# A two-layer hybrid encoder step on one core: the cached keys and the convolution rows arrive already turned, and scores run one batch ahead

## What is computed

```python
def _fox_sample(q, k, v, logf, ck, cv, clogf):
    k_all = jnp.concatenate([ck.astype(k.dtype), k], axis=1)      # 512 cached keys, 16 new ones
    v_all = jnp.concatenate([cv.astype(v.dtype), v], axis=1)
    ...
    sc = jnp.einsum('bqhd,bkhd->bhqk', q, k_all, preferred_element_type=jnp.float32) * scale
    sc = sc + cq[..., None] - c_t[:, :, None, :]
    sc = jnp.where(mask, sc, -jnp.inf)
    p = jax.nn.softmax(sc, axis=-1)
    return jnp.einsum('bhqk,bkhd->bqhd', p.astype(v_all.dtype), v_all)

def _layer(...):
    ...
    y_conv, new_conv = _causal_dwconv(u, conv_hist, conv_w)
    x = x + jnp.concatenate([o_ret, o_fox, o_conv], axis=-1) @ w_out
    gate_c, new_ffn = _causal_dwconv(gate_pre, ffn_hist, ffn_conv_w)
    x = x + (jax.nn.silu(gate_c) * (h2 @ w_up)) @ w_down
```

## Time and profile before

| | |
|---|---|
| median of 3 runs | 1590.44 us (1589.42 to 1591.83) |
| the profiled execution, its own time | 1592.12 us |
| its span in the profile | 1590.3 us |
| busy: TensorE | 1569.7 us, 99% |
| busy: VectorE, ScalarE, POOL | 1073.3, 684.6, 398.4 us |
| chain that ended last | TensorE 90%, VectorE 5% |
| DMA | 168.06 MB, mean 106 GB/s |

### The profile page before, as it was taken

One profiled execution on the slowest core, in us unless ns is written; L12 is line 12 of the kernel. 1 busy time (PEld: TensorE's weight loads), 2 busy tenths in 40 slices (PEclk: granted clock), 3 DMA queues, 4 the chain that ended last, 5 costly groups with the idle time before them and its releaser, 6 DMA issues.

```text
span 1590.3 us, 29061 instructions
## 1 busy us (share of the span) xinstructions
PE 1569.7 (99%) x10196; PEld 1375.7 (87%) x10196; DVE 1073.3 (67%) x1847; ACT 684.6 (43%) x1280; POOL 398.4 (25%) x505
## 2 busy tenths in 40 slices
PE   8999999999999999999999999999999999999998
PEld 6878896789999999999888788877899999999997
DVE  4445447539988888888644552675499888878885
ACT  4224327426444444444433233463365444444442
POOL 1113200003433333333112140000044333333330
PEclk9999999999999999999999999999999999999999
DMA  7213455722222233222242235455213222222222
GB/s 230 80 49 91 138 156 192 264 80 67 80 86 86 79 86 88 89 85 73 77 108 67 70 82 180 171 197 203 80 55 117 84 89 79 79 79 79 80 78 72
DMA packets 118872, 168.06 MB, mean 106 GB/s; under 512 B 28261, under 2 KB 80175, under 8 KB 114624
## 3 DMA queue, kind: packets, MB, share of 16 engines
q1 hardware_dynamic: 118648, 166.95, 33.7%
q10 hardware_dynamic: 146, 0.07, 0.0%
HBM read 157.11 MB, written 9.89 MB: 105 GB/s over the span
## 4 chain that ended last, share of the span: by engine, by line
PE 90%; DVE 5%; issue 1%; ACT 1%; DMA 1%; DVEq 1%; POOL 0%; POOLq 0%; SPq 0%; ACTq 0%
PE bank L2239 85%; PE bank L2301 5%; DVE wlo L1538 1%; DVE pf L1898 0%; DMA raw<-in_w_gate 0%; DVE pf L1911 0%; DMA raw<-in_w_in 0%; DVE wlo L1552 0%; DVE xn L1590 0%; DVE x L2026 0%; DVE gulo L1562 0%; DVE gact L2056 0%; DVE hlo L1562 0%; POOLq L1123 0%; POOL s L1121 0%
## 5 line engine op out<-in xcount | busy, mean ns | idle before, releaser
L2239 PE MATMUL bank<-whi,hhi 128*128 128x512 f32 x560 | 225.1, 402 | 0.9 <-DVE hlo L1562 0.6
L2239 PE MATMUL bank<-whi,hlo 128*128 128x512 f32 x560 | 219.3, 392 | 0.0
L2239 PE MATMUL bank<-wlo,hhi 128*128 128x512 f32 x560 | 218.9, 391 | 0.0
L2239 PE MATMUL bank<-hhi,whi 128*128 128x320 f32 x640 | 198.7, 310 | 0.8 <-DVE hlo L1562 0.8
L2239 PE MATMUL bank<-hhi,wlo 128*128 128x320 f32 x640 | 197.8, 309 | 0.0
L2239 PE MATMUL bank<-hlo,whi 128*128 128x320 f32 x640 | 197.6, 309 | 0.0
L1538 DVE TENSOR_TENSOR wlo<-raw,whi 128x1024 fp32r<-128x1024 f32 x80 | 100.0, 1251 | 109.4 <-ACT whi L1156 108.0
L2239 PE MATMUL bank<-whi,guhi 128*128 128x512 f32 x440 | 171.7, 390 | 0.4 <-DVE gulo L1562 0.4
L2239 PE MATMUL bank<-wlo,guhi 128*128 128x512 f32 x440 | 171.3, 389 | 0.0
L2239 PE MATMUL bank<-whi,gulo 128*128 128x512 f32 x440 | 171.3, 389 | 0.0
L2026 DVE TENSOR_TENSOR x<-x,bank 128x512 f32<-128x512 f32 x220 | 142.7, 680 | 29.4 <-PE bank L2239 28.5
(11 more groups left out here) (310 smaller groups left out, 3605.1 us busy)
## 6 DMA issues: line engine op xcount, KB each, us to landing
raw<-in_w_in SPq DMA_DIRECT2D x52, 512.0 KB, 3.9
raw<-in_w_gate SPq DMA_DIRECT2D x44, 512.0 KB, 3.8
raw<-in_w_down SPq DMA_DIRECT2D x44, 512.0 KB, 3.6
vb<-in_cache_fox_v SPq DMA_DIRECT2D x14, 1024.0 KB, 6.8
raw<-in_w_up SPq DMA_DIRECT2D x24, 512.0 KB, 3.8
gains<-in_w_up SPq DMA_DIRECT2D x20, 512.0 KB, 3.7
raw<-in_w_out SPq DMA_DIRECT2D x16, 512.0 KB, 5.7
kb<-in_cache_fox_k SPq DMA_DIRECT2D x6, 1024.0 KB, 4.9
```

The costliest lines, as they stand in the source:

```text
L2239: return pe.matmul(out, lhsT=lhsT, rhs=rhs, start=start, stop=stop, skip_group_check=True)
```

## The change

1. The host lays out `cache_fox_k` with head dimension on partitions and positions along the row, still 8 KB of one batch per partition. `keys_turned`, `key_copy`, `kT` as a destination and `k0` go; `scores` read the loaded buffer itself.
2. History and taps come as one array in the layout of `taps`: one load replaces four, and the transposes, the bank and ScalarE's copy go. In the second layer SP waits for the last history copies of the first (`gpad_hist`) before it.
3. On TensorE scores run one batch further on: `scores(1)` comes before the loop, and step n has `turned(n)`, `scores(n+1)`, `values(n)`. `ss`, `sn` and `pt` alternate between two banks each. VectorE's steps are put as maxima of n+1, then scaling of n−1; ScalarE has exps(0) and exps(1), then in each step the copy of `pt` and exps(n+1).
4. Keys get five homes (the old place of `kT` is one), values four (`vr` lies under `bcr`, the prompt's bias). SP's loads and their waits follow: K3 a little earlier, K4 when the last prompt output is full, then K5, V4, K6, V5, K7, V6, V7 each when the buffer's former content was used. The splits of the `w_out` slabs wait for `so` of batch 3, not 2; ScalarE's come one step later, VectorE's stay in steps 5 to 7 but stand behind the scaling.

```diff
-K_HOME = (0, 1, 2, 3, 0, 1, 0, 1)
-V_HOME = (0, 1, 2, 0, 1, 0, 1, 0)
+K_HOME = (0, 1, 2, 3, 4, 0, 2, 4)
+V_HOME = (0, 1, 2, 3, 0, 2, 3, 0)
...
     if n < NB:
-        jobs += [(("kt", n, p), K_BANKS[(4 * n + p) % 3]) for p in range(4)]
-        jobs += [(("ss", n), 2), (("sn", n), 4)]
+        jobs += [(("ss", n), (2, 0)[n % 2]), (("sn", n), (4, 3)[n % 2])]
     if 1 <= n <= NB:
-        jobs += [(("pt", n - 1), 6), (("so", n - 1), 5)]
+        jobs += [(("pt", n - 1), (6, 1)[n % 2]), (("so", n - 1), 5)]
     if n >= 1:
         jobs.append((("po", n), 7))
...
-        def key_home(n, p_):
-            return kT[:, p_, :] if n > 0 else k0[:, p_, :] if p_ < 2 else kT[:, p_ - 2, :]
-
         oc = ccs
-        kcache = (kb, kbo, kx, ky)
-        vcache = (vb[:, 0], vb[:, 1], vx[:, :, :])
+        kcache = (kb, kx, kbo, ky, kT)
+        vcache = (vb[:, 0], vx[:, :, :], vb[:, 1], vr[:, :, :])
...
-                sp.dma_start(rows[0:16, 0:CW], one("state_conv").rearrange("o b w c -> (o b w) c")).then_inc(rows_in, 16)
-                sp.dma_start(rows[0:16, CW:], one("state_ffn_conv").rearrange("o b w c -> (o b w) c")).then_inc(rows_in, 16)
-                sp.dma_start(rows[16:19, 0:CW], one("conv_w").rearrange("o w c -> (o w) c")).then_inc(rows_in, 16)
-                sp.dma_start(rows[16:19, CW:], one("ffn_conv_w").rearrange("o w c -> (o w) c")).then_inc(rows_in, 16)
+                if l > 0:
+                    sp.wait_ge(gpad_hist, l * PAIRS)
+                sp.dma_start(taps[:, :, :], one("taps").rearrange("o p n -> p (o n)").rearrange("p (c n) -> p c n", c=NCT)).then_inc(taps_in, 16)
...
                 load_k(l, 0)
                 load_v(l, 0)
                 B.wait_full(sp, ("cb_", 1, 1), l)
-                load_k(l, 2)
-                load_v(l, 2)
+                load_k(l, 1)
+                load_v(l, 1)
                 sp.wait_ge(u_last, l + 1)
                 B.wait_taken(sp, ("fs", 5, 1), l)
                 load_bcr(3)
+                load_k(l, 3)
                 sp.wait_ge(cat_lo, l * CATS + 1)
-                load_k(l, 1)
-                load_v(l, 1)
-                load_k(l, 3)
+                load_k(l, 2)
+                load_v(l, 2)
 
                 def next_pb(b):
                     sp.wait_ge(smax, l * NB + b - 3)
                     load_pb(b)
 
-                B.wait_full(sp, ("kt", 0, 3), l)
+                B.wait_taken(sp, ("fs", len(fox_units()) - 1, 1), l)
+                load_v(l, 3)
+                B.wait_full(sp, ("fo", 3), l)
                 load_k(l, 4)
+                B.wait_full(sp, ("ss", 0), l)
+                load_k(l, 5)
                 next_pb(4)
                 B.wait_full(sp, ("so", 0), l)
-                load_v(l, 3)
-                B.wait_full(sp, ("kt", 1, 3), l)
-                load_k(l, 5)
+                load_v(l, 4)
                 next_pb(5)
-                B.wait_full(sp, ("so", 1), l)
-                load_v(l, 4)
+                B.wait_full(sp, ("ss", 2), l)
+                load_k(l, 6)
                 next_pb(6)
-                B.wait_full(sp, ("kt", 4, 3), l)
-                load_k(l, 6)
-                B.wait_full(sp, ("so", 3), l)
+                B.wait_full(sp, ("so", 2), l)
                 load_v(l, 5)
                 next_pb(7)
-                B.wait_full(sp, ("kt", 5, 3), l)
+                B.wait_full(sp, ("ss", 4), l)
                 load_k(l, 7)
+                B.wait_full(sp, ("so", 3), l)
+                load_v(l, 6)
                 B.wait_full(sp, ("so", 4), l)
-                load_v(l, 6)
-                B.wait_full(sp, ("so", 5), l)
                 load_v(l, 7)
 
...
-                evac("taps", taps[:, :, :], l, view=lambda b: b[:, 0:NCT * NTAP].rearrange("p (c n) -> p c n", c=NCT))
...
-                    if n == NU + 2:
-                        evac(("kt", 0, 2), key_home(0, 2), l)
...
-                for n in range(STEPS):
-                    step(n)
+                def exps(n):
+
+                    act.wait_ge(smax, l * NB + n + 1)
+                    o = SB + 8 * (n % 3)
+                    for c0, n_, acc in ((0, PAST, 3), (PAST + NS * n, NS, 4)):
+                        act.activation(ps[:, n % 2, c0:c0 + n_], ps[:, n % 2, c0:c0 + n_], ACT.Exp, scale=-1.0,
+                                       bias=col(o + 2), accum_out=col(o + acc)).then_inc(sexp, 1)
+
+                for n in range(2):
+                    exps(n)
+                for n in range(1, NB + 1):
+                    evac(("pt", n - 1), pTs[:, (n - 1) % 2, 0:512], l)
+                    if n in (5, 6, 7):
+                        B.wait_full(act, ("so", 3), l)
+                        upto(WO + n - 5, l)
+                    if n + 1 < NB:
+                        exps(n + 1)
                 B.wait_taken(act, ("po", STEPS - 1), l)
...
+                def scaled(n):
+                    o = SB + 8 * (n % 3)
+                    dve.wait_ge(sexp, l * 2 * NB + 2 * n + 2)
+                    dve.tensor_tensor(col(o + 5), col(o + 3), col(o + 4), ALU.add)
+                    dve.drain()
+                    dve.reciprocal(col(o + 6), col(o + 5))
+                    dve.drain()
+                    key = ("so", n)
+                    B.wait_full(dve, key, l)
+                    dve.tensor_scalar(ob[:, n % 2, :], bank[B.bank(key)][:, 0:P], col(o + 6), None,
+                                      ALU.mult).then_inc(B.free[B.bank(key)], 1)
+
+                maxima(0)
+                maxima(1)
+                heads_lo(3)
+                for n in range(1, STEPS):
+                    turned_rows(n)
+                    if n + 1 < NB:
+                        maxima(n + 1)
+                    if n <= NB:
+                        scaled(n - 1)
                     if n in (5, 6, 7):
-                        B.wait_full(dve, ("so", 2), l)
+                        B.wait_full(dve, ("so", 3), l)
                         upto(WO + n - 5, l)
-                    if n == 1:
-                        heads_lo(3)
-                    if n >= 1:
...
-                    for p_ in (1, 3) if n == 1 else (2, 3):
-                        B.wait_taken(pe, ("kt", n, p_), l)
+                    wait_cached(pe, k_in, K_HOME, n, l)
                     B.wait_room(pe, past, l)
                     for p_ in range(4):
                         r = slice(32 * p_, 32 * p_ + 32)
-                        ins = mm(bp[r, :], qbd[:, u, r], key_home(n, p_), True, True)
+                        ins = mm(bp[r, :], qbd[:, u, r], kcache[K_HOME[n]][:, p_, :], True, True)
                     fill(ins, past)
 
                 units = fox_units()
...
+                scores(1)
                 for n in range(1, NB):
                     turned(n)
-                    scores(n)
+                    if n + 1 < NB:
+                        scores(n + 1)
                     values(n)
 
```

153 lines of the change are left out of this document (51 added, 102 removed).

## The result

The changed kernel takes 1580.1 us (median of four runs, 1577.8 to 1582.0) where the kernel before took 1590.96 beside it: ratio 0.9932, interval 0.9915 to 0.9949. That is 10.9 us less, where 24.5 were forecast, and outside the range of 1557 to 1577. The profiled execution has a span of 1579.2 us.

A forecast was written before the change was run, and what follows sets the result against it. TensorE, busy 99%, was taken as the bound. 12.1 us a layer gained less 1.5 for transfers, twice, plus 3.3 for the rows, gave 24.5 us less: 1565.9 us, own range 1562 to 1570, wider range 1557 to 1577.

The forecast's parts named there:

- Filter and history rows: Both layers: 24 transposes leave TensorE's queue, 1.65 us a layer, 3.3 us in all.
- Batch 0's key transposes: Start of the cached-batch stage: two transpose groups and a stall before the scores go, 2.5 us less a layer.
- The loop of 3.5 us: Batches 1 to 7: VectorE's maximum and scaled output, then TensorE's transpose and scores, make 3.5 us a batch, against TensorE's 3.0.
- Transfers: Key and value loads inside the stage: at 365 GB/s K7 lands at 290.4, wanted at 289.0; 1.5 us lost a layer.
- The tail: Stage's end: slab splits delay the last steps; scores(6) end at 19.1, first w_out product starts at 28.4 after scores(0).
- Rival B: Cached-batch stage bound by transfers: at 300 GB/s K7 lands 5.7 us late; 1574 us, chance 0.22.
- Rival D: Cached-batch stage: short waits in every batch drop TensorE's clock to the lower level; 1590 us, chance 0.03.
- Rival E: Downstream of the stage: a late slab split or norm gives back half the gain; 1578 us, chance 0.05.
- A: Cached-batch stage: TensorE stays the bound at 3.0 us a batch, K7 ends the stage; 1560 us, chance 0.13.
- C: Cache loads each have the queue alone for 6.8 us, first w_out product 9.3 us late; 1606 us, chance 0.02.

The follow-up runs named there:

- a_nobias: The changed kernel without the loads of the bias tables of batches 4 to 7 (1.05 MB less a layer; measuring only): 1562.3 us.
- c_split: c_v3 with VectorE's split of the second w_out slab moved from the step of batch 6 to that of batch 7: 1561.3 us.
- d_distinct: c_split with the four early bias tables read from 128 different 2 KB rows of the key cache (measuring only): 1560.2 us, one run.
- b_inline: The changed kernel without the look-ahead: each batch's scores computed in its own step again: 1571.0 us.
- b_early: The changed kernel with bias tables 4 to 7 loaded early into their own place, values 3 loaded inside the stage: 1565.6 us.
- b_homes: b_early with keys 5, 6 and 7 in the places of keys 1, 0 and 2, so asked for sooner: 1564.2 us.
- d_same: c_split with the early tables read from 8 rows of the key cache, each for 16 partitions (measuring only): 1562.2 us, one run.
- b_rows8k: b_homes with scratch tables stored head by head, so one load with 8 KB rows brings all four: 1569.6 us.
- d_spread: c_split with the same scratch rows cut by head: eight loads of 16 partitions x 4 rows in place of four: 1562.1 us.
- c_v3: b_homes with values 3 ahead of values 4 in SP's order: 1563.7 us.
- a_order: The changed kernel with only SP's order different: tables 5 and 7, keys 6 and 7 no longer behind value loads 4 and 5: 1575.7 us.
- a_half: The changed kernel loading half of keys 5 to 7 and values 4 to 7, 3.7 MB less a layer (measuring only): 1561.9 us.
- c_rows: The changed kernel with tables 4 to 7 read from 128 different 2 KB rows of the key cache (measuring only): 1567.1 us.

## Why the prediction was wrong

- **Filter and history rows**, −3.3 us: 3.5 measured alone. Right.
- **Batch 0's key transposes**, −2.5 a layer: the end of the first scores moved from 269.79 to 264.68, 5.1 us; 2.4 of it was there before the stage (1.65 and a start 0.76 us earlier), so 2.7. Right. (The 267.25 of the prediction, and with it K4's 268.3, leave out the rows' 1.65 us: K4 went out at 265.8. Nothing rests on it, since the loads and the need for them shift together.)
- **The loop of 3.5 us**: periods of 3.2 to 3.7 until the transfers break in, 3.53 from scores to scores (272.01 to 275.54), and the whole stage without them: a_nobias takes 30.1 and 29.6 us, c_split 30.0, d_distinct 28.7 in layer 1, where the prediction's 28.4 from the end of the first scores is 29.4 by these marks. Right, and by the mechanism that was named: TensorE goes on when the scaled output is done.

```profile
274.66 0.35 DVE L1983 TENSOR_SCALAR ob<-bank,small 128x128 f32<-128x128 f32 x1
```
```profile
275.12 0.30 PE L2280 MATMUL bank<-const,ps 128*128 128x128 f32 x1 [0.28 <-issue]
```

The wait is 0.28 us, not 0.5, since TensorE's own work came to 3.2 us and not 3.0 (271.01 to 274.18). That the sum hits 3.53 is luck in part: it has 0.17 + 0.11 + 0.09 us from the scaled output to the scores, the trace 0.11 + 0.42, as one more transpose stands behind the wait; and it has 0.36 us ahead of the maximum and 1.02 for the scores, the trace 0.28 and 0.94. One reading was wrong, without consequence: the 3.0 us up to the first transposes of probabilities were TensorE's other work and not "maxima plus exponential"; the change shows 2.7 (264.68 to 267.39).
- **Transfers**, the step that failed. The prediction gave K7 1.5 us; the run shows 4.3 for K7, 2.3 and 2.0 for two tables (VectorE's waits), 0.4 to 0.8 for K6, and a clock that fell behind these waits. K7 alone sets the end of the stage. Scores(7) start 29.8 us behind the end of the first scores (264.68 to 294.49), where the prediction's loop wanted them at 21.8: 8.0 us late, of which TensorE shows 4.3 as its wait for K7, since the late tables had held it up before. Three things in it were mis-sized. (a) The rate, 365 GB/s: I took it from a stretch of whole-row loads and priced 1.05 MB of tables by their bytes. Measured is 306 to 325 with tables in the queue, and 357 to 424 in the full windows of a_nobias, which has none. The trace of before had a row for it, in a microsecond in which a table was alone in the queue, and it wasn't read:

```profile
274.00:275.00 1.00, 1.00 (x22) 0.51 (x17) 0.00 (x0) 0.17 (x1) 0.00 (x0) 1.00 0.33 121
```

A table at 121 GB/s takes 2.2 us, not 0.7. (b) The order: I let loads land one behind the other. By 294.4, when K7 was whole, the windows (220 GB/s from 265 to 270, then those above) add up to 8.9 MB, 1.5 MB more than the 7.34 up to K7: values 6, which SP asks for at 281.5, and perhaps values 7 and a slab (289.2 and 290.8) shared the queue with it. With both, an estimate from these rows closes: 7.85 MB of whole rows at 424 GB/s and four tables at 2.2 us take 27.2 us; from SP's issue of K4 at 265.8 to K7 whole it was 28.6. (c) I asked of the queue only when K7 lands; VectorE's need for tables 5 to 7 was never set against SP's order, in which table 5 stands behind values 4. In the change this lies under the wait for K7; it would bind as soon as K7 came in time.
- **The tail.** The prediction's sum has it (the stage after the last scores), but not what it means: whatever delays the last key load is paid in full, and then two value groups follow. This is where the change loses to b_inline, whose last scores start no sooner behind its first ones (31.3 us, against 30.8).
- **Rival B** (transfers, 1574 us) named the mechanism and was too small: it has K7 5.7 us late at 300 GB/s, measured is 8.0 us behind the time that the loop wanted. It had left out that later loads share the queue with K7, and the clock. The HBM limit of about 358 GB/s that the Trainium skill gives (DMA: Bandwidth & Descriptors, section Bandwidth) decided nothing here: whole rows move at 424 in the window above, well over it, and with tables the queue stays well under it. **Rival D** (the clock) came true in part, behind the long waits and not from the short ones of each batch: from its last scores on, the change takes 7.68 us where the same instructions take 6.34 at a clock of 1.0 (b_early, b_homes): 1.3 us a layer. The lower clock from 286 to 288 lies ahead of the wait for K7, which hides it. The rule of the Trainium skill that was weighed there (TensorE: Matmul & The Clock Gate, section A second HAM failure mode) tells of short idles; the waits of 0.3 to 0.6 us in each batch left the clock at 1.00 until 285, so for these the trace does not agree. **Rival E** fell: from the first w_out product of layer 1 to the end of the span the change takes 495.8 us, as before. **A** and **C** didn't come.

The sum closes: 3.5 for the rows, 2 × 2.7 for batch 0, 0.5 + 1.0 for the stages make 10.4 of the 10.9 us.

## What to carry to other kernels

When work is taken away that covered a stream of loads, price the loads one by one at the rate of their own kind, from a moment in which such a load is alone in the queue, and set each against the time at which it is wanted; bytes over the best rate is a bound, not an estimate. A load that spreads a few rows over many partitions is dear out of proportion (about 2 us for 262 KB alone in the queue here): put it where the queue is idle. A look-ahead on the side that waits for data adds its depth to the tail: check what is still to be done once the last load is in.

## What the runs showed of the hardware

- A load of 8 rows of 2 KB, each for 16 partitions, moved 125 to 187 GB/s at a DMA share near 0.5 (c_split, d_same), one with rows of 8 KB 115 and 123 (b_rows8k), and one cut so that the share was 1.0 moved 126 to 143 (d_spread); 128 different rows of 2 KB moved 334 (d_distinct). In a full queue such tables bring the rate from 357 to 424 GB/s (a_nobias) down to 306 to 325 (the change). Whether rereading alone does it, and why, no run here tells.
- TensorE stood still in the middle of groups of equal products with no semaphore to wait for; the profile calls it "issue". In layer 0 of ten of the runs such a stop stands at the same place of the program, behind the 24th of the 32 value products of batch 5: 0.95 us in a_nobias, d_distinct and d_spread, 0.96 in c_split, 1.04 in b_early (with the queue at a share of 0.06), 1.24 in c_v3, 1.51 in d_same, 2.57 in a_order, 2.59 in a_half, 3.41 in c_rows (share 1.0). A full queue alone doesn't make it long: a_nobias has a share of 1.05 there. In the kernel before, all "issue" stops of TensorE come to 1.0 us. A fixed place would fit the loading of the program itself: the profile has a DMA queue "instruction", and it moved a packet of 0.02 MB within the stops of c_rows and a_half. That this is what TensorE waited for, no run tested.
- The clock after an idle stretch isn't settled by its length alone: after 3.41 us of idle time c_rows kept 1.00, after 2.59 us a_half fell to 0.75, and after 1.73 us b_homes to 0.66 (each the mean of 5 us). The windows of c_rows, then a_half:

```profile
285.00:290.00 5.00, 1.59 (x43) 1.12 (x37) 1.35 (x8) 1.10 (x4) 0.00 (x0) 1.00 0.96 384
```
```profile
285.00:290.00 5.00, 3.17 (x38) 1.96 (x42) 2.08 (x7) 2.30 (x6) 0.00 (x0) 0.75 0.47 166
```
